# Scattering the experts' rows in the tokens' order, without the empty slots

## The reference, cut to what matters

```python
def hierarchical_moe(h, wg_router, bg_router, we_router, be_router, w_gate, w_up, w_down):
    ...
    g_sel = jnp.argmax(g_logits, axis=-1)
    ...
    top_v, top_i = lax.top_k(e_in, TOP_K_EXPERTS)       
    top_w = jax.nn.softmax(top_v, axis=-1) * g_w
    ...
    for g in range(N_GROUPS):
        a = jnp.einsum('nd,edf->nef', hf, w_gate[g])     # 1024 -> 256
        b = jnp.einsum('nd,edf->nef', hf, w_up[g])
        hid = jax.nn.silu(a) * b * gates[:, g, :, None].astype(hf.dtype)
        out = out + jnp.einsum('nef,efd->nd', hid, w_down[g])   # 256 -> 1024
    ...
x = x + hierarchical_moe(...)
```

## Time and profile before

| | |
|---|---|
| median of 3 runs | 1781.07 us (1778.8 to 1783.66) |
| profiled execution, its own time | 1780.79 us |
| its span in the profile | 1778.9 us |
| TensorE busy, share of the span | 87% |
| VectorE / ScalarE / GpSimd | 41% / 24% / 2% |
| mean granted TensorE clock | 0.931 |
| DMA: bytes, mean rate | 214.41 MB, 121 GB/s |

### The profile page before, as it was taken

The page is one execution under the profiler, slowest core; times in us unless marked ns, Lnnn a source line. Parts: engine busy times, 40 slices in busy tenths (PEclk is TensorE's granted clock), DMA queues, the critical chain, the costliest instruction groups (busy, mean ns, idle before and its releaser), DMA issues. The chain is left out here.

```text
span 1778.9 us, 14121 instructions
## 1 busy us (share of the span) xinstructions
PE 1539.3 (87%) x4914; PEld 731.1 (41%) x4914; DVE 731.3 (41%) x1670; ACT 421.0 (24%) x671; POOL 28.7 (2%) x45
## 2 busy tenths in 40 slices
PE   5999999999999999999958997757978787778882
PEld 2455555555555455444423442323435533222220
DVE  2377767767776500010222883443311423111113
ACT  2334343444442400000010304043112430000000
POOL 0000000000000000000000000000000001000001
PEclk8999999999999999999979998868988898898896
DMA  5121112211011411230300110102204045999995
GB/s 220 48 95 60 48 36 80 74 60 60 24 36 49 165 59 48 71 106 34 133 26 25 49 48 0 54 1 94 107 12 166 17 180 189 418 429 429 428 431 213
DMA packets 37791, 214.41 MB, mean 121 GB/s; under 512 B 4961, under 2 KB 5857, under 8 KB 30690
## 3 DMA queue, kind: packets, MB, share of 16 engines
q1 hardware_dynamic: 33554, 198.42, 29.6%
q0 software_dynamic: 3600, 13.11, 2.0%
q10 hardware_dynamic: 576, 2.10, 0.3%
HBM read 201.03 MB, written 12.58 MB: 120 GB/s over the span
## 5 line engine op out<-in xcount | busy, mean ns | idle before, releaser
L407 PE MATMUL gla_proj<-hT,weight_slots 128*128 128x512 f32 x896 | 394.7, 596 | 7.1 <-PEq L278 7.1
L407 PEld LDWEIGHTS gla_proj<-hT,weight_slots 128*128 128x128 f32 x896 | 168.0, 191 | 203.3 <-issue 203.3
L2199 PE MATMUL ex_p_gu<-weight_slots,ex_rowsT 128*64 128x512 f32 x512 | 137.5, 690 | 44.8 <-DMA weight_slots<-in_w_gu 42.0
L868 PE MATMUL bl_p<-hT,weight_slots 128*128 128x512 f32 x256 | 114.7, 601 | 1.8 <-PEq L158 1.8
L2199 PEld LDWEIGHTS ex_p_gu<-weight_slots,ex_rowsT 128*64 128x64 f32 x512 | 41.2, 155 | 130.8 <-issue 81.4
L2305 DVE TENSOR_TENSOR ex_hidden<-ex_silu,ex_p_gu 128x256 f32<-128x256 f32 x16 | 6.7, 421 | 177.2 <-ACT ex_silu L2260 177.2
L868 PEld LDWEIGHTS bl_p<-hT,weight_slots 128*128 128x128 f32 x256 | 48.8, 192 | 63.0 <-issue 62.5
L561 ACT ACTIVATE gla_level_decay<-gla_level_decay 128x1024 f32<-128x1024 f32 x56 | 59.1, 1057 | 39.3 <-DVE gla_level_decay L690 38.8
L905 ACT ACTIVATE bl_sig<-bl_p 128x512 f32<-128x512 f32 x16 | 9.6, 598 | 215.4 <-PE bl_p L868 215.4
L433 PEld LDWEIGHTS gla_level<-gla_level_q,gla_level_k 128*128 128x128 f32 x448 | 55.0, 192 | 11.5 <-issue 11.5
L2220 PE MATMUL ex_p_Y<-weight_slots,ex_hiddenT 128*64 128x512 f32 x256 | 58.5, 598 | 0.8 <-DVE ex_hiddenT L2309 0.8
(11 more groups left out here) (367 smaller groups left out, 1996.4 us busy)
## 6 DMA issues: line engine op xcount, KB each, us to landing
weight_slots<-in_w_gu SPq DMA_DIRECT2D x32, 2048.0 KB, 16.6
weight_slots<-in_w_dn SPq DMA_DIRECT2D x16, 2048.0 KB, 11.9
weight_slots<-in_w_gla SPq DMA_DIRECT2D x40, 512.0 KB, 3.6
weight_slots<-in_w_merge SPq DMA_DIRECT2D x32, 512.0 KB, 3.8
weight_slots<-in_w_out SPq DMA_DIRECT2D x16, 512.0 KB, 3.3
expert_rows<-ex_y SPq DMA_DIRECT2D x16, 512.0 KB, 12.3
weight_slots<-in_w_v SPq DMA_DIRECT2D x3, 2048.0 KB, 8.0
weight_slots<-in_w_u SPq DMA_DIRECT2D x8, 512.0 KB, 6.3
```

What stands on the lines that cost most here:

```text
L407: last = nc.tensor.matmul(pj[:, n % 2, :], lhsT, rhs, start=(k == 0), stop=(k == KT - 1))
L868: last = nc.tensor.matmul(pp[:, m % 4, :], core.slot(slot)[:, k, :], src[:, k, :], start=(k == 0), stop=(k == KT - 1))
L2199: last = nc.tensor.matmul(pG[rows, e, :], hgT[:, k, rows], gu[e][k // 4][:, x, k % 4, :], start=(k == 0), stop=(k == KT - 1))
```

## The change

1. `core.Y` has 1024 rows in place of 16384, in the order (token, choice). The numbers in `ix` become 2 x token + choice, made with an offset: the table `ids` holds 2 x token + choice - 2T, and an add of 2T brings it back, so that an empty slot, which sums to 0, holds 2T = 1024, out of bounds.
2. A second table `ixg` is `ix` shifted right by one, the token number; an empty slot holds 512. Gathers use it with `bounds_check=T - 1, oob_is_err=False`, which leaves out the rows that are out of bounds. The tile of the gathered rows is cleared once in the front (`hg_clear`).
3. The stores of SyncE go. POOL scatters the 128 rows of `ys` to `core.Y` by `ix`, with the empty ones left out in the same way. It issues gather(u+3), scatter(u), waits for the end of scatter(u-1) and gives `y_free`, on which the copies of y now wait, and goes on with gather(u+4). It also issues gathers for units 16 to 18, all empty in round 0.
4. The waits for the end of the scatters, and then the load of `most` and the branch, are on POOL.
5. `pos` goes. The combine loads, for each block of 128 tokens, 1 MB with a plain DMA from SyncE (8 KB a partition).

```diff
 # front: gather of unit 0, clearing, tables
+                pool.wait_ge(hg_clear, 1)
                 pool.wait_ge(ix_ready, 1)
                 nc.gpsimd.indirect_dma_start(out=hg[:, 0, :], out_offset=None, in_=core.h_rows[:],
-                                             in_offset=bass.IndirectOffsetOnAxis(ap=ix[:, 0:1], axis=0)).then_inc(hg_in[0], 16)
+                                             in_offset=bass.IndirectOffsetOnAxis(ap=ixg[:, 0:1], axis=0),
+                                             bounds_check=T - 1, oob_is_err=False).then_inc(hg_in[0], 16)
...
-                chain(nc.vector.memset(ix[:, P:P + 1], 0))
+                nc.vector.memset(ixg[:, P:P + 3], T)
+                chain(nc.vector.memset(hg[:], 0.0))
+                dve.engine_nop().then_inc(hg_clear, 1)
...
-                nc.vector.tensor_copy(ix[:, 0:PAIRS], pL[:, 0:PAIRS]).then_inc(ix_ready, 1)
+                chain(nc.vector.tensor_scalar(ix[:, 0:PAIRS], pL[:, 0:PAIRS], 2.0 * T, None, ALU.add))
+                nc.vector.tensor_scalar(ixg[:, 0:PAIRS], ix[:, 0:PAIRS], 1, None, ALU.arith_shift_right).then_inc(ix_ready, 1)
...
-                chain(nc.vector.scalar_tensor_tensor(out=rank[:], in0=unit[:], scalar=float(CAP), in1=slot[:],
-                                                     op0=ALU.mult, op1=ALU.add))
-                chain(nc.vector.tensor_copy(pos[:], rank[:]))
...
-                nc.vector.tensor_copy(ix[:, PAIRS:P], pR[:, PAIRS:P])
+                chain(nc.vector.tensor_scalar(ix[:, PAIRS:P], pR[:, PAIRS:P], 2.0 * T, None, ALU.add))
+                nc.vector.tensor_scalar(ixg[:, PAIRS:P], ix[:, PAIRS:P], 1, None, ALU.arith_shift_right)
 # experts, SyncE
-                def store(dst, e, value):
-                    sp.wait_ge(ya, value)
-                    sp.wait_ge(yb, value)
-                    sp.dma_start(dst, ys[:, e]).then_inc(y_out[e], 16)
...
 # experts, POOL
                 def gather(u, e):
-                    col_ = ix[:, u:u + 1] if isinstance(u, int) else ix[:, bass.ds(u, 1)]
                     pool.wait_ge(t_done, u + 1)
-                    chain(nc.gpsimd.tensor_copy(ixc[:, e:e + 1], col_))
+                    chain(nc.gpsimd.tensor_copy(ixc[:, e:e + 1], column(ixg, u)))
                     nc.gpsimd.indirect_dma_start(
                         out=hg[:, e, :], out_offset=None, in_=core.h_rows[:],
-                        in_offset=bass.IndirectOffsetOnAxis(ap=ixc[:, e:e + 1], axis=0)).then_inc(hg_in[e], 16)
+                        in_offset=bass.IndirectOffsetOnAxis(ap=ixc[:, e:e + 1], axis=0),
+                        bounds_check=T - 1, oob_is_err=False).then_inc(hg_in[e], 16)
+
+                def scatter(u, e):
+                    own = ixc[:, 2 + e:3 + e]
+                    chain(nc.gpsimd.tensor_copy(own, column(ix, u)))
+                    pool.wait_ge(ya, u + 2)
+                    nc.gpsimd.tensor_tensor(ixc[:, 4:5], own, own, ALU.add)
+                    pool.wait_ge(yb, u + 2)
+                    nc.gpsimd.tensor_tensor(ixc[:, 5:6], own, own, ALU.add)
+                    nc.gpsimd.indirect_dma_start(
+                        out=core.Y[:], out_offset=bass.IndirectOffsetOnAxis(ap=ixc[:, 2 + e:3 + e], axis=0),
+                        in_=ys[:, e, :], in_offset=None, bounds_check=2 * T - 1, oob_is_err=False).then_inc(y_out[e], 16)
+
+                def y_is_out(e, value):
+                    pool.wait_ge(y_out[e], value)
+                    nc.gpsimd.tensor_tensor(ixc[:, 6:7], ixc[:, 2 + e:3 + e], ixc[:, 2 + e:3 + e], ALU.add).then_inc(y_free, 1)
...
-                    with pool.Fori(0, n // 2) as i:
-                        for e in range(2):
-                            u = pool.snap(i * 2 + (first + e + 1))
-                            gather(u, 1 - e)
+                    gather(first + 3, 1)
+                    scatter(first, 0)
...
+                    with pool.Fori(0, n // 2 - 1) as i:
+                        u = pool.snap(i * 2 + (first + 1))
+                        out = pool.snap(i * 16 + 16 * (h + 1))
+                        gather(u + 3, 0)
+                        scatter(u, 1)
+                        y_is_out(0, out)
+                        gather(u + 4, 1)
+                        scatter(u + 1, 0)
+                        y_is_out(1, out)
                         chain.restart()
...
 # experts, ACT and DVE alike
-                    act.wait_ge(y_out[e], w)
+                    act.wait_ge(y_free, u + 1)
...
 # combine
-            more = pool.value_load(most[0:1, 0:1], min_val=0, max_val=T)
-            with pool.If(more > CAP):
-                gather(core.Y[:])
-            with pool.Else():
-                gather(core.Y[0:PAIRS * P])
+        @block.sync
+        def _(sp):
+            for n in range(NB):
+                sp.dma_start(g[:, n], rows[n]).then_inc(got[n], 16)
```

More of the change, by code:

```diff
@@ L1821, in project_stage, with moe_front_stage @@
         core.w_n[base + j] += 16
-def moe_front_stage(core, omT, x_rows, gate, pos, most, ix, hg, hg_in):
+def moe_front_stage(core, omT, x_rows, gate, most, ix, ixg, hg, hg_in):
     nc, dram, xT = core.nc, core.dram, core.xT
@@ L2149, in _, with column @@
                         run(r)
[L2150 to L2153, removed]
             @block.gpsimd
             def _(pool):
+                def column(src, u):
+                    return src[:, u:u + 1] if isinstance(u, int) else src[:, bass.ds(u, 1)]
                 def gather(u, e):
-                    col_ = ix[:, u:u + 1] if isinstance(u, int) else ix[:, bass.ds(u, 1)]
@@ L2165, in run @@
+                def y_is_out(e, value):
+                    pool.wait_ge(y_out[e], value)
+                    nc.gpsimd.tensor_tensor(ixc[:, 6:7], ixc[:, 2 + e:3 + e], ixc[:, 2 + e:3 + e], ALU.add).then_inc(y_free, 1)
                 def run(r):
                     first, n = r * PAIRS, PAIRS
-                    with pool.Fori(0, n // 2) as i:
-                        for e in range(2):
-                            u = pool.snap(i * 2 + (first + e + 1))
-                            gather(u, 1 - e)
-                        chain.restart()
+                    h = r * (n // 2)
+                    gather(first + 3, 1)
+                    scatter(first, 0)
+                    if not isinstance(r, int):
+                        y_is_out(1, h * 16)
+                    chain.restart()
+                    with pool.Fori(0, n // 2 - 1) as i:
[7 more added lines that the diff above has]
+                        y_is_out(1, out)
+                        chain.restart()
+                    u = first + n - 1
+                    gather(u + 3, 0)
+                    scatter(u, 1)
+                    y_is_out(0, (h + n // 2) * 16)
+                    chain.restart()
@@ L2172, in _ @@
                 chain = Chain(pool, ix_ready)
+                gather(1, 1)
+                gather(2, 0)
+                chain.restart()
                 run(0)
+                pool.wait_ge(y_out[1], 16 * (PAIRS // 2))
+                for e in range(2):
+                    pool.wait_ge(hg_in[e], 16 * (PAIRS // 2 + 2 - e))
                 with pool.If(pool.value_load(most[0:1, 0:1], min_val=0, max_val=T) > CAP):
@@ L2176, in _ @@
                         run(r)
+                    pool.wait_ge(y_out[1], 16 * (SLOT_ROUNDS * PAIRS // 2))
+                    for e in range(2):
+                        pool.wait_ge(hg_in[e], 16 * (SLOT_ROUNDS * PAIRS // 2 + 2 - e))
             @block.tensor
@@ L2348, in _, with combine_stage @@
                         run(r)
-def combine_stage(core, x_rows, gate, pos, most, out):
+def combine_stage(core, x_rows, gate, out):
     nc = core.nc
+    rows = core.Y.rearrange("(n p c) d -> n p c d", p=P, c=2)
     with (nc.sbuf_tensor("cb_g", [P, NB, 2, D], F32) as g, nc.Block() as block):
@@ L2356, in combine_stage @@
         summed, stored, dch = core.sem("summed"), core.sem("stored"), core.sem("dve_chain")
[L2358 to L2373 removed]
+        @block.sync
+        def _(sp):
+            for n in range(NB):
+                sp.dma_start(g[:, n], rows[n]).then_inc(got[n], 16)
+            for n in range(NB):
+                sp.wait_ge(summed, n + 1)
+                sp.dma_start(out[n * P:(n + 1) * P, :], x_rows[:, n]).then_inc(stored, 16)
+            sp.wait_ge(stored, 16 * NB)
         @block.vector
@@ L2383, in _ @@
                                                in1=x_rows[:, n], op0=ALU.mult, op1=ALU.add).then_inc(summed, 1)
-        @block.sync
-        def _(sp):
-            for n in range(NB):
-                sp.wait_ge(summed, n + 1)
-                sp.dma_start(out[n * P:(n + 1) * P, :], x_rows[:, n]).then_inc(stored, 16)
-            sp.wait_ge(stored, 16 * NB)
 def load(core, pairs):
@@ L2487, in build @@
                 core.recycle()
-                moe_front_stage(core, omT, x_rows, gate, pos, most, ix, hg, hg_in)
-            experts_stage(core, most, ix, hg, hg_in)
```

(4 more changed lines are left out.)

76 lines of the change are left out of this document (28 added, 48 removed).

## The result

The changed kernel takes 1770.41 us (median of four runs, 1769.6 to 1771.26), against 1781.8 us for the kernel before in its comparison: a ratio of 0.9937, 95% interval 0.9923 to 0.9952. Forecast were 1772.6 us and "faster". The profiled execution took 1770.0 us with a span of 1768.1 us, 10.8 us less than the span before.

A forecast was written before the change was run, and what follows sets the result against it. The 16 DMA engines were taken to bound the experts' stretch, 1509 to 1735 us. Stretch -6.7, work ahead +0.45, tail -1.9 sum to -8.2 us, from 1780.8 to 1772.6 us; range 1761 to 1784 us.

The forecast's parts named there:

- The DMA-bound stretch: Mixture of experts, 1509 to 1735 us: leaving out empty slots takes 6.7 us off, period about 16.6 us.
- the middle between two bounds: Rows per engine in the stretch: 156, between 104 (-14.7 us) and 208 (+1.2 us); chance 0.45.
- the 151 of the forecast: Rows on the fullest engine in the stretch's 26 transfers by the skill's swizzle rule, giving -7.5 us.
- Even dealing: Rival for the stretch: left-out rows spread evenly over the DMA engines, -14.7 us there, 1764.6 us; chance 0.24.
- nothing saved: Rival for the stretch: fullest engine loses no rows, or left-out rows cost their slot, +1.2 us, 1780.5 us; chance 0.25.
- Ahead of the stretch: Front before the experts' stage: longer making of row lists adds 0.45 us; the 1.77 us tile clear stays hidden.
- POOL in the stretch: POOL's gathers and scatters in the experts' stretch: later gathers still land in time, with 26 us for them; no cost.
- the slower rival: Experts' stretch: late scatters hold up copies of y from a 31 us landing on, some 1788 us; chance 0.06.
- The tail: From last copy of y to the end: scatter +2.0, load and branch +1.6, combine -5.5, together -1.9 us.
- The load and branch: Tail: load of `most` and branch come on POOL after the last wait instead of under the store, +1.6 us.
- The combine: Four plain 1 MB loads replace eight indirect gathers: 15.3 us in place of 20.8, -5.5 us.
- the loads keep ahead: Combine: the last load lands after 12.1 us and is needed at 12.7 us, so DVE does not wait.

The follow-up runs named there:

- experiment 1: Kernel of indirect transfers alone, by which slots hold a row: scatters wait 2.91 us for slots 0-3 with 32-35, 2.31 for slots 0-7, 3.11 for a full set.
- 2: Changed kernel with each expert's rows dealt (spread) over its 64 slots: 1765.01 us, ratio 0.9900.
- 3: Changed kernel with rows packed as badly as possible, an expert's first eight in slots 0-3 and 32-35, and so on: 1783.84 us, ratio 1.0014.
- run 4: Changed kernel with all slots moved: an empty slot gathers the last token's row and scatters it behind the 1024 real rows: 1781.75 us, ratio 0.9994.
- 8: Kernel with rows dealt over the slots, with `ix` and `ixg` each made by one operation out of PSUM: 1765.11 us, ratio 0.9906.
- 11: Changed kernel with empty slots left out in the scatters only; gathers are full, empty slots gathering the last token's row: 1773.81 us, ratio 0.9962.
- run 9: Kernel with rows dealt, `ix` and `ixg` by one operation each, `most` loaded early, last scatter and gather waits on SyncE: 1762.23 us, ratio 0.9893.
- Experiment 7: Changed kernel with each scatter awaited right after its issue, before the next gather: 1788.26 us, ratio 1.0034.
- 5: Kernel with rows dealt over the slots, with POOL's load of `most` moved to the start of its stage: 1761.74 us, ratio 0.9883.

## Why the prediction was right, and where its terms were off

**The DMA-bound stretch: mechanism right, term too small, -11.7 us for -6.7.** The step was to take the middle between two bounds because no row told the dealing. Experiments 1 to 3 show the dealing: fours with a partner 32 further on. The Trainium skill ("DMA: Bandwidth & Descriptors", The descriptor swizzle) gives that rule for GpSimd's transfers to 128 partitions; experiment 1 agrees, with 3.97 against 3.00 us for gathers and 2.91 against 2.31 us for scatters. Counted exactly, the fullest engine has 139 rows in the 26 transfers of the stretch; the 151 of the forecast was scaled up from the 16 units, not counted over the transfers that lie in it. From 200 to 139 rows are 61, at 0.153 to 0.160 us 9.3 to 9.8 us. The rest, some 2 us, does not come from rows: the second distance was 20.32 us before at a clock of 0.83 and in run 4, with all rows moved, 18.34 at 1.00. At most 1.1 us of this is the clock's (experiment 4); what set the clock and what delayed the weights there is not shown, and the forecast had no term for it. What the forecast named as signs came: a period of 16.32 us (forecast 16.6), 6.5 MB less in the stretch (425 GB/s over 226.56 us and 418 over 214.89; forecast 7), a rate under 429. The DMA share was to be near 0.97 and stood at 1.01: the view's share does not show idle engines at this level; only the packed kernel's 0.96 does.

**Even dealing (1764.6 us) and nothing saved (1780.5 us)** were both refuted as descriptions of this kernel and both then made: dealing the rows gave 1765.0, packing them 1783.8 us. The 3.3 us between 1780.5 and 1783.8 are the lower clock at the start (2.4 us in the changed kernel), the tail (0.85 us less gain than forecast there) and a stretch 1.6 us longer than before in place of 1.2, less the 0.45 us that the front did not cost.

**Ahead of the stretch: +0.45 us, measured +0.33** from the list to the presets, and the clear of 1765 ns was all but hidden: the multiply behind it began 2.29 us after the front's start, for 2.10. Yet the front as a whole took 64.97 for 64.98 us: its part up to the list was 0.34 us shorter, which no run explains. And a term was missing. The first turn and the first `gate_up` ran at a lower granted clock, 0.72 for 1.00 over 12 us, and cost +2.4 us. The slow `gate_up` was there in all ten profiles with the change and in neither of the kernel before; the slow turn came and went with small shifts of the front (runs 4, 8, 11), the `gate_up` did not. TensorE's idle time ahead of the last list matmuls and ahead of the first turn was 3.13 and 1.09 us before, 3.33 and 1.22 in the changed kernel; runs 8 and 9, at 3.13 and 1.15, still had the slow `gate_up`. The cause is open.

**POOL in the stretch: right.** The slack of 26 us for a gather was ample: landings were 13.8 us in the median and 14.7 at most, and TensorE did not wait for one. Scatters landed in 10.6 us (11.4 at most) against the 31 us from which the slower rival decides; it is refuted for this kernel: in the tile view all 32 copies of y waited for TensorE and none for `y_free`. Experiment 7 shows that the reasoning by slack is sound but that its size hung on the order of two instructions.

**The tail: -1.05 us for -1.9.** From the last copy to the combine's first instruction went 5.63 to 9.21 us: +3.6, as forecast, but by two errors that cancel. The scatter was to land 2.0 us later than the store; it was issued 0.7 us later and landed in 3.3 us, while the last store of before took 4.6, not the 2.6 of the lone store I used. So it came 0.6 us sooner. The load and branch were to cost 1.6 us; from landing to SyncE's load 5.1 us went by, 1.0 before, +4.1. Priced were the two instructions, not what else follows a wait on POOL before the stage can end; with the load early and the waits on SyncE (run 9) 2.35 us are left. The combine: 1748.91 to 1765.05 is 16.1 us for 20.8, -4.7 against -5.5. The step that failed is "the loads keep ahead": the last landed 12.2 us after its issue at 1750.23, and DVE waited 1.05 us for it. It landed 13.5 us after the combine's start, for 12.1 forecast, and was needed at 12.5.

**The sum.** -11.7, +2.4, -1.05 and -0.5 upstream are -10.8 us of span; forecast -8.2. The 5.0 us by which the stretch gained more, and the 2.4 us of clock and 0.85 us of tail that were lost, partly cancel: that the median came within 2.2 us of the forecast is in part luck.

## What to carry to other kernels

When a transfer leaves rows out, count what the fullest DMA engine still moves, not the bytes: the same 2048 rows cost 1765 or 1784 us by their slots alone. Where slots may be chosen, spread the rows so that each four slots and the four 32 further on get an equal part. A change of queue moves a stage's last wait to another engine; price what comes after that wait from a row in which that engine waits last. And test an order of waits by its slack: here one scatter's landing, 14 us, was the difference between a gain and a loss.

## What the runs showed of the hardware that I had not expected

- A row that is out of bounds in an indirect transfer is not dropped: the records hold a packet of 4 bytes and 9 ns for it, and a scatter with no row at all waits 1.87 us against 3.11 us for a full one (experiment 1).
- The granted clock at the start of the experts' stage was 0.72 in the changed kernel and 1.00 in the one before, with the same matmuls in the same order; and in the second distance 0.83 before, 0.90 after, and 1.00 when all rows moved. The first place is worth 2.4 us against the change, the second at most 1.1 us for it.
- A load of 2 MB raises its semaphore in 16 steps. In the stretch between the first and the last step of one load of weights lay 2.6 to 3.4 us before and 1.5 to 2.0 us with all rows moved (run 4); in the changed kernel 1.2 us for the first and, from the second of the eleven periods on, 4.5 to 6.3 us (worked out from the semaphore records).

The best version is the changed kernel with its rows dealt over the slots, 1761.7 to 1765.1 us (runs 2, 5, 8 and 9), 18 to 21 us under the kernel before in their comparisons.
